# Weights of the seven-product pairs placed 32 bytes off a 64-byte line in a two-block transformer kernel

## The reference

```python
# first block
h = h + (jax.nn.silu(hn @ w_gate[l]) * (hn @ w_up[l])) @ w_down[l]

# second block, twice
def swiglu(h, w_gu, w_down):
    a, b = jnp.split(h @ w_gu, 2, axis=-1)
    return (jax.nn.silu(a) * b) @ w_down
```

## Time and profile before

| what | us |
|---|---|
| median of three runs (2004.41 to 2006.53) | 2005.5 |
| span of the profiled execution, first to last instruction | 2004.3 |
| PE busy in it | 1982.4 |
| PEld busy | 1717.1 |
| DVE busy | 1236.5 |
| POOL busy | 905.8 |
| ACT busy | 898.6 |

### The profile page before, as it was taken

The page is one execution under the profiler, slowest core; times in us unless marked ns, Lnnn a source line. Parts: engine busy times, 40 slices in busy tenths (PEclk is TensorE's granted clock), DMA queues, the critical chain, the costliest instruction groups (busy, mean ns, idle before and its releaser), DMA issues.

```text
span 2004.3 us, 32457 instructions
## 1 busy us (share of the span) xinstructions
PE 1982.4 (99%) x11622; PEld 1717.1 (86%) x11622; DVE 1236.5 (62%) x1937; ACT 898.6 (45%) x1605; POOL 905.8 (45%) x458
## 2 busy tenths in 40 slices
PE   9999999999999999999999999999999999999998
PEld 7788788878999988899998888887777888999887
DVE  4675885346788787877768774463552247777111
ACT  4334444344566522556652252225663245666322
POOL 3344323326577655544445434443224445444443
PEclk9999999999999999999999999999999999999999
DMA  6243212212333286333338635322222223333321
GB/s 209 90 152 106 74 64 83 86 33 94 106 105 105 95 314 247 101 115 105 105 95 326 237 120 149 116 95 85 68 70 85 89 89 95 105 105 105 103 98 63
DMA packets 67246, 234.71 MB, mean 117 GB/s; under 512 B 7632, under 2 KB 9040, under 8 KB 66640
## 3 DMA queue, kind: packets, MB, share of 16 engines
q1 hardware_dynamic: 66432, 232.29, 35.3%
q10 hardware_dynamic: 720, 1.15, 0.2%
HBM read 225.54 MB, written 2.10 MB: 114 GB/s over the span
## 4 chain that ended last, share of the span: by engine, by line
PE 94%; DVE 3%; ACT 1%; issue 1%; DMA 0%; POOL 0%; SPq 0%; POOLq 0%; DVEq 0%; ACTq 0%
PE bank L2254 12%; PE bank L2255 12%; PE bank L2260 12%; PE bank L2433 9%; PE bank L2434 9%; PE bank L2437 9%; PE bank L2378 5%; PE bank L2379 5%; PE bank L2384 5%; PE bank L2228 1%; PE bank L2230 1%; PE bank L2229 1%; PE bank L2552 1%; PE bank L2560 1%; PE bank L2553 1%; PE bank L2870 1%
## 5 line engine op out<-in xcount | busy, mean ns | idle before, releaser
L538 POOL TENSOR_TENSOR wlo<-raw,whi 128x1024 fp32r<-128x1024 f32 x233 | 579.9, 2490 | 807.7 <-ACT whi L657 807.4
L657 ACT ACTIVATE whi<-raw 128x1024 fp32r<-128x1024 f32 x233 | 245.8, 1057 | 475.0 <-PE bank L2384 217.7
L2254 PE MATMUL bank<-xh,whi 128*128 128x512 f32 x764 | 302.0, 395 | 1.2 <-DVE xl L1355 0.9
L2255 PE MATMUL bank<-xl,whi 128*128 128x512 f32 x764 | 297.7, 390 | 0.0
L2378 PE MATMUL bank<-hh,whi 128*128 (+1 forms) x480 | 186.9, 389 | 1.0 <-ACT whi L657 1.0
L2379 PE MATMUL bank<-hl,whi 128*128 (+1 forms) x480 | 186.8, 389 | 0.0
L2260 PE MATMUL bank<-xh,wlo 128*128 128x512 f32 x736 | 181.6, 389 | 0.0
L2254 PEld LDWEIGHTS bank<-xh,whi 128*128 128x128 f32 x764 | 143.5, 188 | 34.9 <-issue 4.7
L2255 PEld LDWEIGHTS bank<-xl,whi 128*128 128x128 f32 x764 | 143.5, 188 | 29.5 <-issue 0.7
L2260 PEld LDWEIGHTS bank<-xh,wlo 128*128 128x128 f32 x736 | 138.1, 188 | 28.9
L2434 PE MATMUL bank<-xl,whi 128*128 128x256 f32 x648 | 162.5, 283 | 0.0
(11 more groups left out here) (396 smaller groups left out, 4510.0 us busy)
## 6 DMA issues: line engine op xcount, KB each, us to landing
raw<-units SPq DMA_DIRECT2D x341, 512.0 KB, 3.7
ada_w<-ada_rows SPq DMA_DIRECT2D x72, 512.0 KB, 5.6
h<-x_t SPq DMA_DIRECT2D x8, 256.0 KB, 5.3
out_t<-h SPq DMA_DIRECT2D x8, 256.0 KB, 2.1
raw<-units SPq DMA_DIRECT2D x4, 256.0 KB, 4.5
mem_in<-mem_t SPq DMA_DIRECT2D x1, 1024.0 KB, 11.2
turned_q<-proj SPq DMA_DIRECT2D x4, 256.0 KB, 5.1
dec<-decays SPq DMA_DIRECT2D x4, 256.0 KB, 4.7
```

What stands on the lines that cost most here:

```text
L538: pool.tensor_tensor(wlo[:, j % 2 * UNIT:(j % 2 + 1) * UNIT], raw[:, j * UNIT:(j + 1) * UNIT], whi[:, j % 2 * UNIT:(j % 2 + 1) * UNIT].bit ...
L657: act.activation(whi[:, v % 2 * UNIT:(v % 2 + 1) * UNIT], raw[:, slot * UNIT:(slot + 1) * UNIT], ACT.Copy).then_inc(hi_ready, 1)
L2254: mm(bank[:, 0:n], wh, chunk(rhs[0], t, n), start=t == 0, stop=False)
L2255: mm(bank[:, 0:n], wh, chunk(rhs[1], t, n), start=False, stop=False)
```

## The change

The change adds no instruction and moves none: each engine issues the same instructions in the same order, with other addresses. `SLOT` is the new length of a slot of `whi` and `wlo`, 64 bytes more than a unit. A plain unit starts at its slot's start, as before. A half unit of a pair is written and read 32 bytes further on (`pair_half`). The sums 1 and 2 and the high part of sum 3 start 32 bytes later, and have 64 bytes more behind them so that they fit. `w_t3_low` is not edited. All the buffers behind `whi` move up by 128 to 384 bytes, which are multiples of 64. In the new build `w_t3_low` is again 32 bytes past a line, as now are all weights of the pairs. `raw` and all activations stay on multiples of 64.

```diff
 UNIT = 8 * P
+SLOT = UNIT + 16
...
-        raw, whi, wlo = sb("raw", 4 * UNIT), sb("whi", 2 * UNIT, f32r), sb("wlo", 2 * UNIT, f32r)
+        raw, whi, wlo = sb("raw", 4 * UNIT), sb("whi", 2 * SLOT, f32r), sb("wlo", 2 * SLOT, f32r)
...
-        ssum, rstd = sb("ssum", T), sb("rstd", T)
+        ssum = sb("ssum", T)
+        sb("ssum_trail", 16)
+        rstd = sb("rstd", T)
...
-        side = sb("side", 12 * 256)
+        side = sb("side", 12 * 256 + 16)
...
-        side_at = arena_at - 12 * 1024
+        side_at = arena_at - 12 * 1024 - 64
+        half_line = 1 / 32
...
-        w_t1 = at("w_t1", 8, 8 * P, f32r, base=side_at)
-        w_t2 = at("w_t2", 0, 8 * P, f32r, base=xn_at)
-        w_t3_high = at("w_t3_high", 4, 4 * P, f32r, base=xn_at)
+        w_t1 = at("w_t1", 8 + half_line, 8 * P, f32r, base=side_at)
+        w_t2 = at("w_t2", half_line, 8 * P, f32r, base=xn_at)
+        w_t3_high = at("w_t3_high", 4 + half_line, 4 * P, f32r, base=xn_at)
...
+        def pair_half(buf, slot, half):
+
+            o = slot * SLOT + 8 + half * 4 * P
+            return buf[:, o:o + 4 * P]
...
-        T_HI = {1: w_t1[:, 0:4 * P], 2: w_t2[:, 0:4 * P], 3: w_t3_high[:, :], 4: unit_half(whi, UP, 0)}
-        T_LO = {1: w_t1[:, 4 * P:8 * P], 2: w_t2[:, 4 * P:8 * P], 3: w_t3_low[:, :], 4: unit_half(wlo, UP, 0)}
+        T_HI = {1: w_t1[:, 0:4 * P], 2: w_t2[:, 0:4 * P], 3: w_t3_high[:, :], 4: pair_half(whi, UP, 0)}
+        T_LO = {1: w_t1[:, 4 * P:8 * P], 2: w_t2[:, 4 * P:8 * P], 3: w_t3_low[:, :], 4: pair_half(wlo, UP, 0)}
...
-                pool.tensor_tensor(wlo[:, j % 2 * UNIT:(j % 2 + 1) * UNIT], raw[:, j * UNIT:(j + 1) * UNIT],
-                                   whi[:, j % 2 * UNIT:(j % 2 + 1) * UNIT].bitcast(f32), ALU.subtract).then_inc(lo_ready, 1)
+                pool.tensor_tensor(wlo[:, j % 2 * SLOT:j % 2 * SLOT + UNIT], raw[:, j * UNIT:(j + 1) * UNIT],
+                                   whi[:, j % 2 * SLOT:j % 2 * SLOT + UNIT].bitcast(f32), ALU.subtract).then_inc(lo_ready, 1)
...
-                    product(left(banks[LEFT_BANK]), unit_half(whi, GATE, 1), unit_half(wlo, GATE, 1), x12,
+                    product(left(banks[LEFT_BANK]), pair_half(whi, GATE, 1), pair_half(wlo, GATE, 1), x12,
...
-                o = slot * UNIT + t * P
+                o = slot * SLOT + t * P
                 wh, wl = whi[:, o:o + P], wlo[:, o:o + P]
```

More of the change, by code:

```diff
@@ L568, in gate_first @@
                     slot = (u1 + 2 * r) % 4
-                    pool.tensor_tensor(unit_half(wlo, GATE, 0), unit_half(raw, slot, 0), unit_half(whi, GATE, 0).bitcast(f32),
+                    pool.tensor_tensor(pair_half(wlo, GATE, 0), unit_half(raw, slot, 0), pair_half(whi, GATE, 0).bitcast(f32),
                                        ALU.subtract).then_inc(first_lo, 1)
@@ L574, in gate_second @@
                     slot = (u1 + 2 * r) % 4
-                    pool.tensor_tensor(unit_half(wlo, GATE, 1), unit_half(raw, slot, 1), unit_half(whi, GATE, 1).bitcast(f32),
+                    pool.tensor_tensor(pair_half(wlo, GATE, 1), unit_half(raw, slot, 1), pair_half(whi, GATE, 1).bitcast(f32),
                                        ALU.subtract).then_inc(lo_ready, 1)
@@ L580, in up_second @@
                     slot = (u1 + 2 * r + 1) % 4
-                    pool.tensor_tensor(unit_half(wlo, UP, 1), unit_half(raw, slot, 1), unit_half(whi, UP, 1).bitcast(f32),
+                    pool.tensor_tensor(pair_half(wlo, UP, 1), unit_half(raw, slot, 1), pair_half(whi, UP, 1).bitcast(f32),
                                        ALU.subtract).then_inc(lo_ready, 1)
@@ L656, in high_part @@
                     act.wait_ge(unit_used, v - 1 + 4 * i)
-                act.activation(whi[:, v % 2 * UNIT:(v % 2 + 1) * UNIT], raw[:, slot * UNIT:(slot + 1) * UNIT],
+                act.activation(whi[:, v % 2 * SLOT:v % 2 * SLOT + UNIT], raw[:, slot * UNIT:(slot + 1) * UNIT],
                                ACT.Copy).then_inc(hi_ready, 1)
@@ L852, in gate_first @@
                     slot = raw_in(i, r, 0)
-                    act.activation(unit_half(whi, GATE, 0), unit_half(raw, slot, 0), ACT.Copy).then_inc(first_hi, 1)
+                    act.activation(pair_half(whi, GATE, 0), unit_half(raw, slot, 0), ACT.Copy).then_inc(first_hi, 1)
                 def gate_second(i, g, r):
                     slot = raw_in(i, r, 0)
-                    act.activation(unit_half(whi, GATE, 1), unit_half(raw, slot, 1), ACT.Copy).then_inc(hi_ready, 1)
+                    act.activation(pair_half(whi, GATE, 1), unit_half(raw, slot, 1), ACT.Copy).then_inc(hi_ready, 1)
                 def up_second(i, g, r):
                     slot = raw_in(i, r, 1)
-                    act.activation(unit_half(whi, UP, 1), unit_half(raw, slot, 1), ACT.Copy).then_inc(hi_ready, 1)
+                    act.activation(pair_half(whi, UP, 1), unit_half(raw, slot, 1), ACT.Copy).then_inc(hi_ready, 1)
                 def part_out(r, dst):
@@ L1052, in half_high @@
             def half_high(m, part):
-                o = m * UNIT + part * 4 * P
+                o, w = m * UNIT + part * 4 * P, m * SLOT + part * 4 * P
                 act.wait_ge(raw_loaded[m] if part else opening_in[m], 16)
-                act.activation(whi[:, o:o + 4 * P], raw[:, o:o + 4 * P], ACT.Copy).then_inc(hi_ready if part else opening_hi, 1)
+                act.activation(whi[:, w:w + 4 * P], raw[:, o:o + 4 * P], ACT.Copy).then_inc(hi_ready if part else opening_hi, 1)
             mix_high(0)
@@ L1797, in half_low @@
             def half_low(m, part):
-                o = m * UNIT + part * 4 * P
+                o, w = m * UNIT + part * 4 * P, m * SLOT + part * 4 * P
                 dve.wait_ge(hi_ready if part else opening_hi, m + 1)
-                tt(wlo[:, o:o + 4 * P], raw[:, o:o + 4 * P],
-                   whi[:, o:o + 4 * P].bitcast(f32), ALU.subtract).then_inc(lo_ready if part else opening_lo, 1)
+                tt(wlo[:, w:w + 4 * P], raw[:, o:o + 4 * P],
+                   whi[:, w:w + 4 * P].bitcast(f32), ALU.subtract).then_inc(lo_ready if part else opening_lo, 1)
             mix_low((0,))
@@ L2252, in high_passes @@
                 for t in ts:
-                    wh = whi[:, slot * UNIT + t * P:slot * UNIT + (t + 1) * P]
+                    wh = whi[:, slot * SLOT + t * P:slot * SLOT + (t + 1) * P]
                     mm(bank[:, 0:n], wh, chunk(rhs[0], t, n), start=t == 0, stop=False)
@@ L2259, in low_pass @@
                 for t in range(8):
-                    last = mm(bank[:, 0:n], wlo[:, slot * UNIT + t * P:slot * UNIT + (t + 1) * P], chunk(rhs[0], t, n),
+                    last = mm(bank[:, 0:n], wlo[:, slot * SLOT + t * P:slot * SLOT + (t + 1) * P], chunk(rhs[0], t, n),
                               start=False, stop=t == 7)
@@ L2375, in unit @@
                             for kk, o in tiles:
[L2376 removed]
+                                w0 = par * SLOT + (4 * kk + o) * P
                                 bank = banks[DOWN_BANKS[name][4 * half + o]]
@@ L2449, in gate_first @@
                     n = HN_BEFORE + G * k + g + 1
-                    product(left(banks[GATE_BANK[r]]), unit_half(whi, GATE, 0), unit_half(wlo, GATE, 0), x11,
+                    product(left(banks[GATE_BANK[r]]), pair_half(whi, GATE, 0), pair_half(wlo, GATE, 0), x11,
                             (first_hi, n), (first_lo, n), True).then_inc(five_done, 1)
@@ L2457, in finish @@
                     pe.wait_ge(up_right, GN_BEFORE + G * k + g + 1)
-                    product(left(banks[UP_BANK]), unit_half(whi, UP, 1), unit_half(wlo, UP, 1), s4,
+                    product(left(banks[UP_BANK]), pair_half(whi, UP, 1), pair_half(wlo, UP, 1), s4,
                             (hi_ready, u1 + 2 * g + 2), (lo_ready, u1 + 2 * g + 2), False).then_inc(unit_used, 1)
@@ L2546, in value_units @@
                         for kk in range(2):
-                            w0, c = slot * UNIT + kk * T, 2 * j + kk
+                            w0, c = slot * SLOT + kk * T, 2 * j + kk
                             for s in part:
@@ L2624, in low @@
                     for t in ts:
-                        last = mm(banks[m][:, :], wlo[:, m * UNIT + t * P:m * UNIT + (t + 1) * P], chunk(xh, t),
+                        last = mm(banks[m][:, :], wlo[:, m * SLOT + t * P:m * SLOT + (t + 1) * P], chunk(xh, t),
                                   start=False, stop=t == 7)
```

6 lines of the change are left out of this document (3 added, 3 removed).

## The result

The changed kernel takes 2017.42 us in the median of five runs (2016.85 to 2019.12), the kernel before 2005.5 us beside it. The ratio is 1.0063, with a 95% interval of 1.0052 to 1.0074: 0.6% slower, 11.9 us, where 8.3 us less was forecast. The granted clock is at 1.00 in both, and the profiled spans, 2015.3 and 2004.3 us, differ by 11.0 us.

A forecast was written before the change was run, and what follows sets the result against it. The prediction took TensorE's matmul step as the bound. Its only nonzero term, 8.3 us gained in the pairs, took the span from 2004.3 to 1996.0 us; adding 1.2 us for the median gave 1997.2 us, range 1990.0 to 2006.8.

The forecast's parts named there:

- The bound: Whole kernel: TensorE, busy 1982.4 of 2004.3 us, sets the time through what a matmul costs from start to start.
- The pairs' term: 54 pairs of 84 matmuls: 2.0 ns less per matmul, 154 ns less per pair, 8.3 us gained; chance 0.45.
- The upper end: Pair stages: each load off the line gains 3.4 ns, 14.7 us in all, giving 1990.8 us; chance 0.22 with more.
- The stall: Rival, pair stages: about 4 ns per load returns, 2006.2 us; chance 0.20, shared with the place never having mattered.
- the rival of a ninth line: Pair loads: tiles starting mid-line touch nine 64-byte lines, costing 3.4 ns on each of 4536 matmuls, 2021.6 us; chance 0.08.
- The sign named for a run of four: Profile after, pairs: a run of four low passes on wlo takes about 634 ns where it took 643.
- Its reading: Pair loads: a stall of about 4 ns beside a matmul reading activations, absent where weights lie half a line off.
- Writes off the line: ACT's high parts, DVE's and POOL's low parts: costed at nothing, at worst 1.9 us of DVE time.
- The slack of DVE: Pair stages: tightest handovers found have 1.8 and 2.2 us, pairs get 0.15 to 0.27 us shorter; costed at nothing.
- The plain units, at nothing: 5616 matmuls outside the pairs: starts stay on multiples of 64 bytes, buffers move by multiples of 64, so no cost.
- a rival with slot 1: Plain units on slot 1: 3.4 ns lost on 2808 matmuls, 9.5 us, against 8.3 us gained, 2006.7 us; chance 0.05.

The follow-up runs named there:

- slots_only: The change without its 32-byte offset: slots 64 bytes longer, buffers moved as in the change, pairs' weights on 64-byte lines; 2016.84 us against 2004.25 for the kernel before.
- pair_64: Kernel before, with only the pairs' weights and sums' buffers moved, to distances of 64 or 192, plain units at 0; 1993.38 us against 2004.4.
- arena_32: Kernel before with the arena (hh, hl, yh, yl, oh, memh) 32 bytes further on, which also moves w_t3_low; 2020.32 us in one run.
- offset_only: Kernel before with the pairs' weights and sums' buffers at odd multiples of 32, slots not lengthened, plain units nearly all at distance 0; 1997.15 us against 2004.25.
- slot1_64: Kernel before with slots 64 bytes longer and free bytes behind whi and wlo, so only slot 1 gets another distance, 64; 2016.68 us, one run, beside 2004.8.
- pair_128: Kernel before, with only the pairs' weights and sums' buffers moved, so that every pair weight is at distance 128; 2003.37 us in one run.
- moves_only: Kernel before, slots kept, with wlo 128 and the arena 384 bytes further on and sums' buffers moved as in the change; 2017.57 us, one run, beside 2004.8.

## Why the prediction was wrong

- **The bound** (TensorE's step from matmul to matmul): right. But for the late starts of sum 1 in the first pair stage, which cost under 1 us, the whole 11.9 us is in steps.
- **The pairs' term**, 8.3 us: right in sign and in size, for a wrong reason (next point) and with some luck. Forecast were 9.912 us a pair, which is 2.0 ns a matmul less. Measured were 9.886 us, 2.1 ns less, and 8.2 us over the three stages. The pair gained a sixth more than forecast, and the first stage gave that back. The upper end, 3.4 ns a matmul, would have been too much. The stall did not come back in a stage of 1512 such matmuls, and the rival of a ninth line at 3.4 ns a matmul is out: all these tiles have nine, at 117.7 ns. The sign named for a run of four, 634 ns, went with 2.7 ns a step and not with the 2.0 ns taken, which gives 637; measured are 34.4 us / 54 = 637.
- **Its reading**, that a start in the middle of a 64-byte line frees the load: wrong. `w_t3_low` was the only buffer off a line and also the only one at a distance other than 0. The trace of before can't tell the two apart. slots_only, pair_64 and the loads of `w_t3_low` in arena_32 do: on the line and at another distance than 0 most loads last 188 ns, and in pair_64 the pairs are faster still.
- **Writes off the line**, at nothing: right. offset_only has all these writes, and its time shows no loss by them. DVE's low parts take 692 ns at the median off the line in `w_t3_low` and 691 now in the up slot, where they took 690 on it.
- **The slack of DVE**, at nothing: wrong by a little. The handovers with 1.8 and 2.2 us to spare were read in the second stage. In the first, which the prediction itself calls the fullest for DVE, the one ahead of sum 1 had 0.4 to 0.5 us. It cost the change some 0.7 us and pair_64 some 2.8 us.
- **The plain units, at nothing**: this is the step that failed. I wrote that they still start on a multiple of 64 bytes and that everything behind `whi` moves by whole multiples of 64, and took nothing. Both statements are true and don't matter. What these units had and lost was a distance of 0. I kept a rival with slot 1 at 3.4 ns on 2808 matmuls, 9.5 us. The measured price is 6.8 ns in slot 1 (233.5 against 226.7 in slot1_64), twice that, and it alone would have cost more than the pairs won: 2016.68 us. The moves of `wlo` and the arena, which no rival had, slowed units of slot 0 too: about 20 us in all. The range of 1990.0 to 2006.8 us had no case for it.

The trace of before could have warned. I had seen in the earlier trace rows that 256-column matmuls start free at 117.5 ns and fall in step at 120, and took falling in step for a loss. A plain unit after a break shows the opposite. These are matmuls of 512 columns of the kernel before, all at distance 0:

```profile
81.14 0.39 PE L2254 MATMUL bank<-xh,whi 128*128 128x512 f32 x1
...
82.53 0.39 PE L2254 MATMUL bank<-xh,whi 128*128 128x512 f32 x1
...
84.34 0.39 PE L2260 MATMUL bank<-xh,wlo 128*128 128x512 f32 x1
```

Six steps take 1.39 us, 232 ns each, and the next eight take 1.81 us, 226 ns each. So for 512 columns the pace in step is the fast one and the free pace the slow one, by 5 to 6 ns, and a change that is meant to keep two streams of reads out of step had to be checked on the 5616 plain matmuls (384 of them, on the memory rows, have 256 columns) as well as on the 4536 of the pairs. I had read the plain step only as a mean over runs of eight.

## What to carry to other kernels

Where TensorE's steps are the bound, look at the steps themselves from start to start, also right behind a pause: two paces for the same instruction show that something other than its size sets the pace. Free bytes ahead of a buffer are then a cheap thing to try, but the residue of every pair of operands has to be written down first, since lengthening one buffer moves all that lie behind it. A rule taken from one exceptional buffer should be tried on that property alone before a layout is built on it. And slack has to be read in the fullest stage: here one handover had 2.2 us to spare in one stage and 0.5 us in another.

## What the runs showed of the hardware

The weights here are 128 x 128 tiles and the operands fp32r; no other type was tried. The step between two matmuls depends on the distance between the weights' and the activations' addresses in a partition's row, modulo 256 bytes:

| distance | 512 columns, ns | 256 columns, ns |
|---|---|---|
| 0 | 226.7 | 120.0 |
| 32, 96, 160 or 224 | 233 (224 alone tried) | 117 to 119 over a product |
| 64 | 233.5 | 113.4 or 118 |
| 128 | 232 to 234 | 120.0 or 118.7 (pair_128) |
| 192 | 229 or 233 | 113.4 or 118 |

For 256 columns the distance does not settle the pace: at 64, 128 and 192 each, two were seen at the same distance. Runs of only four low passes behind another distance can be faster than the table, 116 to 117 ns at 128 in moves_only. After a pause or a product at another distance it takes some eight matmuls until the pace of distance 0 is reached.

The Trainium skill, in TensorE: Matmul & The Clock Gate, section on what each phase is for, says that loading the next weights takes nothing from the running matmul, since both have read ports of their own. The runs show that the two are not independent all the same: the addresses of the two alone move the step by 3% at 512 columns and by up to 6% at 256. Whether it is a conflict of the two reads, and where, no run here shows.
